# Two neighbouring steps change places in a softmax loop, and weight splitting moves ahead of follow-up work in a chain of products

## What is computed

```python
for l in range(DEPTH):                       # first block, two layers
    h = rms_norm(x, mix_norm_g[l]); proj = h @ w_in[l]        # then gMLP and attention
    x = x + merged @ w_out[l]                                 # "back"
    x = x + memory_cross_attention(rms_norm(x, xattn_norm_g[l]), ...)   # "ask" is its h @ w_q
    x = x + expert_choice_moe(rms_norm(x, ffn_norm_g[l]), ...)
...
# second block, two layers: layer 0 mixes by rwkv and hyena, layer 1 by neighbourhood attention
h = h + neighbourhood_attention(z, ...) @ na_w_out            # z = rmsnorm(h, na_norm) @ na_w_qkv
h = h + conv_ffn(h, ...)                                      # up, 3-tap convolution, gelu, product, down
h = h + sigmoid(rmsnorm(h, ple_norm) @ w_gate) * (p_i @ w_proj)         # "embedding"

def row_block(i):                            # neighbourhood attention, 16 heads
    s = einsum(q_i, k_win) + bias            # scores of a query against its window
    pr = softmax(s)
    return einsum(pr, v_win)
```

## Time and profile before

| what | value |
|---|---|
| median of 3 runs | 3931.18 us (3930.61 to 3931.74) |
| the profiled execution's own time | 3930.88 us |
| its span, first to last instruction | 3929.6 us |
| PE busy | 3459.3 us, 88% |
| DVE busy | 1848.4 us, 47% |
| ACT busy | 1093.1 us, 28% |
| mean granted TensorE clock | 0.93 of full speed |

### The profile page before, as it was taken

One profiled execution on the slowest core, in us unless ns is written; L12 is line 12 of the kernel. 1 busy time (PEld: TensorE's weight loads), 2 busy tenths in 40 slices (PEclk: granted clock), 3 DMA queues, 4 the chain that ended last, 5 costly groups with the idle time before them and its releaser, 6 DMA issues. The chain is left out here.

```text
span 3929.6 us, 55521 instructions
## 1 busy us (share of the span) xinstructions
PE 3459.3 (88%) x23714; PEld 2422.2 (62%) x23714; DVE 1848.4 (47%) x2870; ACT 1093.1 (28%) x1837; POOL 255.4 (6%) x216
## 2 busy tenths in 40 slices
PE   7689889998878979999797777879999898699999
PEld 6467533332747644333286667747888787478887
DVE  3564433222365542232256455456664643456645
ACT  3353300000344320000133222114343422343333
POOL 1010000000101000000011222100000100000000
PEclk9799989999979989999998888879999997689999
DMA  5022179999202128999821000012222221012222
GB/s 202 11 86 86 72 296 427 427 427 428 102 6 108 65 88 350 428 428 427 343 97 44 2 3 3 3 40 91 107 86 86 86 108 38 27 71 106 96 87 75
DMA packets 49814, 595.84 MB, mean 152 GB/s; under 512 B 5376, under 2 KB 7680, under 8 KB 14080
## 3 DMA queue, kind: packets, MB, share of 16 engines
q1 hardware_dynamic: 49568, 592.29, 37.4%
HBM read 590.17 MB, written 2.10 MB: 151 GB/s over the span
## 5 line engine op out<-in xcount | busy, mean ns | idle before, releaser
L588 PE MATMUL psum<-source_hi,weights_hi 128*128 128x512 f32 (+1 forms) x2352 | 921.4, 392 | 93.9 <-DVE weights_lo L490 69.1
L588 PE MATMUL psum<-source_lo,weights_hi 128*128 128x512 f32 (+1 forms) x2352 | 911.4, 388 | 0.0
L588 PE MATMUL psum<-source_hi,weights_lo 128*128 128x512 f32 (+1 forms) x2352 | 910.8, 387 | 0.0
L588 PEld LDWEIGHTS psum<-source_hi,weights_hi 128*128 128x128 f32 x2352 | 448.6, 191 | 194.6 <-DVE weights_lo L490 83.4
L588 PEld LDWEIGHTS psum<-source_lo,weights_hi 128*128 128x128 f32 x2352 | 449.3, 191 | 90.1 <-issue 2.6
L588 PEld LDWEIGHTS psum<-source_hi,weights_lo 128*128 128x128 f32 x2352 | 448.6, 191 | 89.5
L1392 PE MATMUL psum<-weight_ring_first,branches 128*64 128x512 f32 x2048 | 467.2, 599 | 15.4 <-DMA weight_ring_first<-in_w_up 8.2
L490 DVE TENSOR_TENSOR weights_lo<-weight_ring_second,weights_hi 128x1024 fp32r<-128x1024 f32 (+3 forms) x230 | 288.4, 1259 | 269.8 <-ACT weights_hi L444 269.2
L1392 PEld LDWEIGHTS psum<-weight_ring_first,branches 128*64 128x64 f32 x2048 | 138.5, 137 | 304.8 <-issue 273.9
L444 ACT CAST weights_hi<-weight_ring_second 128x1024 fp32r<-128x1024 f32 (+3 forms) x230 | 228.1, 997 | 246.1 <-PE psum L588 229.4
L1545 DVE TENSOR_TENSOR x<-psum,x 128x512 f32<-128x512 f32 x256 | 164.1, 685 | 202.4 <-PE psum L1425 202.4
(11 more groups left out here) (362 smaller groups left out, 4392.7 us busy)
## 6 DMA issues: line engine op xcount, KB each, us to landing
weight_ring_first<-in_w_gate SPq DMA_DIRECT2D x64, 2048.0 KB, 17.0
weight_ring_first<-in_w_up SPq DMA_DIRECT2D x64, 2048.0 KB, 18.3
lent_weights<-in_w_down SPq DMA_DIRECT2D x64, 2048.0 KB, 17.4
weight_ring_second<-in_ffn_w_up SPq DMA_DIRECT2D x22, 2048.0 KB, 7.6
weight_ring_first<-in_xattn_w_kv SPq DMA_DIRECT2D x8, 2048.0 KB, 7.8
weight_ring_second<-in_ffn_w_down SPq DMA_DIRECT2D x8, 2048.0 KB, 7.6
weight_ring_first<-in_w_in SPq DMA_DIRECT2D x6, 2048.0 KB, 24.3
weight_ring_second<-in_mix_w_in SPq DMA_DIRECT2D x6, 2048.0 KB, 8.1
```

What stands on the lines that cost most here:

```text
L588: ins = pe.matmul(ps, a, b, start=k == 0 and q == 0, stop=k == job.rows // P - 1 and q == 2)
```

## The change

**In `near_attention`.** On VectorE, `row_max(j+2)` is written behind the scaling of step j instead of ahead of it; `keep` now stands behind both. On ScalarE, `exponential(j+1)` instead of `exponential(j+2)` stands ahead of `copy(j)`. TensorE's list is the same as before.

**In `Chain.walk`.** The follow-up work of a unit (`after`) is taken out of `evacuate` into `follow`. For jobs with `lag` 0 a step now reads: empty the unit, split the next weights, follow-up, source tiles, squares. Before, the weights were split at the head of the next step, behind the follow-up, the source tiles and the squares. TensorE's, GpSimd's and SyncE's lists are unchanged.

```diff
-    def walk(self, weights, source, square, root, empty):
+    def walk(self, weights, source, square, root, empty, follow):
...
+        fed = 1
+
+        def feed(below):
+            nonlocal fed
+            while fed < n and self.units[fed].after < below:
+                weights(fed)
+                fed += 1
         for s in range(last + 1):
-            for v in range(max(fed, 1), n):
-                if self.units[v].after >= s:
-                    break
-                weights(v)
-                fed = v + 1
+            feed(s)
...
-            for u, unit in enumerate(self.units):
-                if unit.whole and unit.step == s:
-                    if unit.job.norm is not None and u == unit.job.first:
-                        root(unit.job.norm)
-                    empty(unit)
+            now = [(u, unit) for u, unit in enumerate(self.units) if unit.whole and unit.step == s]
+            for u, unit in now:
+                if unit.job.norm is not None and u == unit.job.first:
+                    root(unit.job.norm)
+                empty(unit)
+            if now and now[0][1].job.lag == 0:
+                feed(s + 1)
+            for u, unit in now:
+                follow(unit)
...
+
+    def follow(self, name, eng, link, unit):
+
+        job = unit.job
         if name in job.after:
...
             for j in range(n):
-                if j + 2 < n:
-                    row_max(j + 2)
                 b = j % 4
                 dve.wait_ge(exp_done, 2 * (j + 1))
                 link(dve.reciprocal(st[:, b, INV], st[:, b, SUM]))
                 for a in range(2):
                     dve.tensor_scalar(prob[:, b, a, :], prob[:, b, a, :], st[:, b, 6 + a:7 + a], None, ALU.mult)\
                         .then_inc(prob_ready, 1)
+                if j + 2 < n:
+                    row_max(j + 2)
...
             exponential(0)
-            exponential(1)
             for j in range(n):
-                if j + 2 < n:
-                    exponential(j + 2)
+                if j + 1 < n:
+                    exponential(j + 1)
                 copy(j)
```

More of the change, by code:

```diff
@@ L375, in slot_free @@
             eng.wait_ge(self.src_used, t + 1 - sum(x.closes for x in self.units[:u]))
-    def walk(self, weights, source, square, root, empty):
-        n, fed = len(self.units), 0
+    def walk(self, weights, source, square, root, empty, follow):
+        n = len(self.units)
         last = max(x.step for x in self.units if x.whole)
@@ L479, in root @@
                 act.wait_ge(self.inverse, norm.inverted)
-        self.walk(weights, source, square, root, lambda unit: self.evacuate("act", act, link, unit))
+        self.walk(weights, source, square, root, lambda unit: self.evacuate("act", act, link, unit),
+                  lambda unit: self.follow("act", act, link, unit))
     def vector(self, dve):
@@ L532, in root @@
                                              op0=ALU.mult, op1=ALU.mult).then_inc(self.rescaled, 1)
-        self.walk(weights, source, lambda q: None, root, lambda unit: self.evacuate("dve", dve, link, unit))
+        self.walk(weights, source, lambda q: None, root, lambda unit: self.evacuate("dve", dve, link, unit),
+                  lambda unit: self.follow("dve", dve, link, unit))
     def gpsimd(self, pool):
```

## The result

| | before | after |
|---|---|---|
| median | 3931.46 us (3930.61 to 3935.38, 4 runs) | 3847.36 us (3839.53 to 3848.98, 4 runs) |
| ratio | | 0.978, 95% interval 0.9763 to 0.9797 |
| span of the profiled execution | 3929.6 us | 3846.0 us |

The change saves 84 us, 2.1%. It is closest to the rival in which the attention runs at 2.4 GHz nearly throughout (3856 us).

The account below looks back on a forecast made before the run. TensorE, busy 88% of the span, was taken as the bound, so only its waits could give time back. Attention 44, end of `back` 14.5 and embedding 6.5 sum to 65 us: 3930.9 - 65 = 3866 us, range 3848 to 3888.

Parts of the forecast that it names:

- the rival in which the attention runs at 2.4 GHz nearly throughout: Attention saves 54 us instead of 44, giving 3856 us in all; chance 0.22.
- The loop of waits now joins j to j+2: Attention: two chains run side by side, so a step costs 1.94 us at the low clock instead of 3.87.
- the 65 to 82 us set as a sign: Attention: expected distance between the transposes of steps 0 and 28 in the changed profile; 119.0 us before.
- The choice of the clock: Attention: a place between low and high clock, step 1.8 us, 75.0 us in all, saving 44 us.
- my upper end: Attention at the high clock: 1.70 us a step, 64.6 us from step 0 to 28, saving 54.4 us.
- The low end: Attention at the low clock: 1.94 us a step, 82.2 us from step 0 to 28, saving 36.8 us.
- `keep` and the value product: Attention, serial costs once a pair: `keep` 1.03 us, value product 3.61 us at low clock, 1.81 at high.
- Behind step 28 little remains: Attention after step 28: little left to overlap, so no gain taken.
- The end of `back`: 5.07 us TensorE hole and 2.2 us low clock go, 7.25 us a layer, 14.5 us in both.
- The embedding: Layer 0 before `qkv`: TensorE's 9.65 us hole shrinks to 3 to 5 us; gain 6.5 us, bounds 4 and 12.5.
- The rest at nothing: Remaining moved work, such as the feed-forward up products where TensorE has no hole, costed at nothing.
- the rival with a slower up step: `weights_lo` holds up the emptying in 88 feed-forward up steps; 3980 us at a 3 us wait; chance 0.03.

Follow-up runs that it names:

- The runs of the two parts: Old kernel with only VectorE's new attention order: 3873.99 us, ratio 0.9849; old kernel with only ScalarE's new attention order: 3933.91 us, ratio 1.0002.
- fillers: Old kernel plus unneeded matmuls ahead of each attention step's transposes, which overwrite them: five a step 3919.42 us, three a step 3903.66 us.

## Why the prediction was off, step by step

- **The loop of waits now joins j to j+2: right.** Steps of 3.87 us became steps of 1.61 us at 2.4 GHz where neither `keep` nor a value product lies in them (1.70 forecast, VectorE's own work). The runs of the two parts place it in VectorE's order, and the exponential issued later costs nothing, as forecast. The transposes wait 0.34, 0, 0.41 and 1.24 us for the scaling in a pair, 0.50 us on the mean, which is the bound that I had set for it. The distance from step 0 to step 28, 62.2 us, missed the 65 to 82 us set as a sign.
- **The choice of the clock: the step that failed.** "I take a place between the two ends", 44 us, assumed that holes come back once the high level is there and pull it down. Holes of 0.34 to 1.24 us in steps of 1.6 to 3.1 us did come back, but the clock fell only once between step 0 and step 28, for about 4 us. Before, with holes of 1.63 us in steps of 3.87, it was back at the low level within 3 to 10 us after each value product that had brought the high one. The granted clock was 0.94. From step 0 to 28 the gain was 119.0 - 62.2 = 56.8 us, a little over my upper end of 54.4. The 26 us that the clock alone gives in the old order show how much hung on this choice. The Trainium skill ("TensorE: Matmul & The Clock Gate", on what is actually happening in the clock gate) has activity release the throttle; the prediction itself said that by this rule alone the sum would hold 54 us, and both the 0.94 here and the 0.99 with fillers agree with it. That the clock still fell now and then behind a hole of 1.24 us, and not where `keep` was moved away, speaks for holes that are not free for the clock, but far cheaper than I took them to be.
- **The low end was worked out wrongly too.** At 1.2 GHz a step is 2.20 us, not 1.94, because TensorE itself is full (4.40 of 4.40 us). I had checked VectorE and ScalarE in numbers and TensorE only as 1.02 + "less than 1.27". The prediction had said that TensorE would have hardly a hole at 1.2 GHz and that the high level should then come more often, and it took the middle all the same.
- **`keep` and the value product: right in kind.** `keep` opens a hole 1.24 - 0.35 = 0.89 us deeper (1.03 forecast), the value product costs 1.48 us (1.81 forecast).
- **"Behind step 28 little remains": mis-sized.** It took 18.95 us before (3440.91 to 3459.86) and 15.60 after: 3.35 us, part of it the last value product at 2.4 GHz, plus 0.9 us ahead of step 0. Taken as 0.
- **The end of `back`: right**, 15.0 us against 14.5, hole and low clock behind it both gone. The stated cause, ScalarE's cast behind the squares, is shown by the run with the cast early on ScalarE alone.
- **The embedding: mis-sized**, 9.3 us against 6.5, inside its bounds of 4 and 12.5. The hole fell to 2.53 us and not to 3 to 5, which is 7.1 us. A small hole ahead of it, 0.92 us at 3117.16, went too, which I had not counted; another, 0.51 us at 3070.15, lies before this stage and is not in the 9.3. The low clock behind the hole stayed: the 36 matmuls from 3114.89 to 3125.33 take 10.44 us instead of 11.04. The 0.7 us that is left is not placed. `weights_lo` fell less than I had hoped where GpSimd adds: 1.75 us beside an addition, 1.49 us beside the end of one, 1.22 us clear of them (in the kernel with the follow-up first). The Trainium skill's rule on the shared port pair ("SBUF — State Buffer") has VectorE and GpSimd shut each other out there, and the trace is in keeping with it: `source_lo` ended at 3093.22, the addition that overlapped it at 3094.37, and `weights_lo` at 3095.45, so each ended about its own undisturbed length (1.3 and 1.2 us) or a little less behind the one before.
- **The rest at nothing: right where it was looked at.** From 2750 to 2950 us TensorE is still busy 200.00 of 200 us, and the rival with a slower up step did not come.

Of the 18.6 us between forecast and result, 12.8 lie between step 0 and step 28 (10.4 are the choice of the clock, 54.4 - 44; 2.4 are costs below the upper end's, above all the value product), 4.3 at the attention's two edges, 2.8 the embedding, 0.5 `back`, less 1.8 us elsewhere.

## What to carry to other kernels

Where a softmax loop is a chain over three engines, look on each engine for the instruction of the next step that stands ahead of the current one: one swap can lay two steps side by side, and then every engine, TensorE at its low clock included, must be checked for being full. Cost such a loop at both levels of the clock. Here TensorE, full at 1.2 GHz for its first 4.40 us, went on at 2.4 GHz for nearly all of the loop, and a forecast half way between the levels was 10 us off; one loop doesn't make that a rule. In a chain of split products put the cast of the next weights ahead of work that waits for the emptied result, and put copies such as `keep` where their engine waits anyway.

## What the runs showed of the hardware

- The clock by itself made a chain over three engines 26% shorter (2.87 us instead of 3.87), though TensorE is only a part of each round: 1.02 us of transposes became 0.63, from the scores to the next maximum 1.27 us became 0.75, and from the reciprocal to the transposes 0.69 us became 0.60.
- Matmuls that do nothing can pay: three a step in idle time gave 30 us in the old order (3903.66 us), five a step only 14 us (3919.42 us), because they themselves filled the step.
- `weights_lo` took 1.20 to 1.23 us clear of GpSimd's additions. Beside one either can be the longer. It took 1.47 to 2.31 us where they overlapped (2.15 us in the kernel before, 2.31 us in the one with the early cast on ScalarE alone). Before `qkv` in that last kernel it took 1.23 us at 3092.46, and the addition that overlapped it took 3.07 us (from 3091.77), where additions that overlapped little took 1.27 to 1.30. That kernel's time was the same as the changed kernel's, so none of this cost time there.
